# An expert's rows at every eighth of its 64 slots, in the place of one slot after the other

## What is computed

```python
def hier_moe(hn, w_group, w_expert, w_gate, w_up, w_down):
    pg = softmax(t @ w_group); g_sel = argmax(pg)            # one of 4 groups
    top_p, top_i = top_k(softmax(el_sel), 2)                 # two of its 8 experts
    comb = sum(one_hot(eid, 32) * w)                         # a weight for each token and expert
    for e in range(32):
        a = silu(t @ w_gate[e]) * (t @ w_up[e])
        out = out + comb[:, e:e + 1] * (a @ w_down[e])
```

## Time and profile before

| | us |
|---|---|
| median of 3 runs | 604.15 |
| lowest and highest | 602.49, 605.76 |
| the profiled execution | 599.2 |
| its span, first to last instruction | 597.4 |

### The profile page before, as it was taken

The page is one execution under the profiler, slowest core; times in us unless marked ns, Lnnn a source line. Parts: engine busy times, 40 slices in busy tenths (PEclk is TensorE's granted clock), DMA queues, the critical chain, the costliest instruction groups (busy, mean ns, idle before and its releaser), DMA issues.

```text
span 597.4 us, 7906 instructions
## 1 busy us (share of the span) xinstructions
PE 517.0 (87%) x2938; PEld 324.1 (54%) x2938; DVE 246.2 (41%) x576; ACT 144.6 (24%) x364; POOL 151.1 (25%) x287
## 2 busy tenths in 40 slices
PE   3597998999999999889995499999978787778895
PEld 3584776777777677568784463334333332333343
DVE  2857668869432465651225522122211101111337
ACT  4542344444635222232111100011000000000110
POOL 5064646203304444651102111111211101100000
PEclk9887997999999999999997589999988988888999
DMA  8521030022005922246926949999999999999884
GB/s 248 206 61 43 19 116 27 2 71 71 2 16 168 320 114 72 70 153 234 418 83 243 420 164 408 412 424 424 425 423 426 425 427 424 425 425 421 363 331 169
DMA packets 35031, 144.75 MB, mean 242 GB/s; under 512 B 5842, under 2 KB 8994, under 8 KB 23216
## 3 DMA queue, kind: packets, MB, share of 16 engines
q1 hardware_dynamic: 27440, 131.58, 55.9%
q0 software_dynamic: 4528, 9.01, 4.2%
q10 hardware_dynamic: 3024, 3.64, 1.8%
HBM read 138.16 MB, written 17.30 MB: 260 GB/s over the span
## 4 chain that ended last, share of the span: by engine, by line
PE 45%; SPq 21%; DVE 15%; issue 5%; ACT 4%; DMA 3%; POOL 2%; ACTq 0%; DVEq 0%; POOLq 0%
PE banks L940 18%; SPq L648 12%; PE banks L1162 7%; SPq L656 6%; DMA w_moe_a<-in_w_up_dram 3%; SPq L729 3%; PE banks L1177 3%; PE banks L1156 2%; PE banks L1115 1%; POOL w_lo L795 1%; PE banks L998 1%; PE banks L1083 1%; PE banks L1078 1%; DVE soft L1720 1%; PE banks L1250 1%
## 5 line engine op out<-in xcount | busy, mean ns | idle before, releaser
L795 POOL TENSOR_TENSOR w_lo<-w_raw,w_hi 128x512 fp32r<-128x512 f32 x52 | 69.1, 1347 | 124.1 <-ACT w_hi L1408 122.4
L1162 PE MATMUL banks<-w_moe_b,xgT 128*64 128x512 f32 x224 | 70.9, 659 | 16.4 <-DMA w_moe_b<-in_w_up_dram 10.5
L1162 PE MATMUL banks<-w_moe_a,xgT 128*64 128x512 f32 x224 | 68.1, 631 | 8.9 <-DMA w_moe_a<-in_w_up_dram 8.9
L940 PE MATMUL banks<-w_hi,xT_hi_a 128*128 128x512 f32 (+4 forms) x140 | 56.6, 404 | 7.0 <-ACT sv L1376 7.0
L1990 DVE SCALAR_TENSOR_TENSOR glu<-banks,wr,glu 128x256 f32<-128x256 f32 x15 | 7.3, 483 | 122.8 <-ACT glu L1537 122.8
L841 POOL DMA_INDIRECT y_d<-y_sb,idx x14 | 14.1, 1005 | 166.7 <-PE banks L1156 111.1
L940 PE MATMUL banks<-w_lo,xT_hi_a 128*128 128x512 f32 (+4 forms) x140 | 53.9, 385 | 0.0
L940 PE MATMUL banks<-w_hi,xT_lo_a 128*128 128x512 f32 (+4 forms) x140 | 53.6, 383 | 0.0
L1162 PEld LDWEIGHTS banks<-w_moe_b,xgT 128*64 128x64 f32 x224 | 22.4, 152 | 57.4 <-issue 54.7
L1537 ACT ACTIVATE glu<-banks,wr 128x256 f32<-128x256 f32 x15 | 7.1, 475 | 155.2 <-PE banks L1162 137.5
L940 PE MATMUL banks<-w_hi,xT_hi_b 128*128 128x512 f32 (+3 forms) x100 | 41.6, 416 | 0.4 <-POOL w_lo L795 0.4
(11 more groups left out here) (273 smaller groups left out, 888.7 us busy)
## 6 DMA issues: line engine op xcount, KB each, us to landing
w_moe_a<-in_w_down_dram SPq DMA_DIRECT2D x20, 1024.0 KB, 25.5
w_moe_a<-in_w_gate_dram SPq DMA_DIRECT2D x16, 1024.0 KB, 18.6
w_moe_a<-in_w_up_dram SPq DMA_DIRECT2D x16, 1024.0 KB, 21.5
w_moe_b<-in_w_gate_dram SPq DMA_DIRECT2D x14, 1024.0 KB, 24.1
w_moe_b<-in_w_up_dram SPq DMA_DIRECT2D x14, 1024.0 KB, 25.8
w_moe_b<-in_w_down_dram SPq DMA_DIRECT2D x12, 1024.0 KB, 24.8
w_raw<-in_w_in_dram SPq DMA_DIRECT2D x36, 256.0 KB, 4.6
y_d<-in_consts_dram SPq DMA_DIRECT2D x9, 512.0 KB, 10.3
```

Source lines behind the costliest of these rows:

```text
L795: nc.gpsimd.tensor_tensor(w_lo[:, s, :], w_raw[:, s, :], w_hi[:, s, :].bitcast(F32), ALU.subtract).then_inc(split, 1)
L940: l = mm(acc2[0:R, j % 2, 0:width], a[:, P * t:P * t + R], w, start=(kk == 0 and q == 0), stop=(kk == KD - 1 and q == 2))
L1162: l = mm(acc[64 * e:64 * e + 64, u, :].rearrange("p (m f) -> p m f", m=2), xgT[:, xu, k, 64 * e:64 * e + 64], units(at_e[e], 2)[:, :, k * ...
```

## The change

The one-hot table is made with another row of constants, `slots`, in the place of `iota`. In the slot s of an expert stands the number s % 8 * 8 + s // 8 + 1, so the row of rank r (from 0) goes to slot (r % 8) * 8 + r // 8: ranks 0 to 7 to slots 0, 8, ... 56, ranks 8 to 15 to slots 1, 9, ... 57, and so on. An expert with 36 rows filled slots 0 to 35; now it fills the slots 0 to 3 of each eight and in four of the eights slot 4 too. The row of constants takes the place of `ones`, and the second half of `counting` is now made by an operation on DVE.

```diff
@@ constants()
-    put("ones", np.ones((P, P)))
+
+    slot = p % CAP
+    put("slots", np.tile(p // CAP * CAP + slot % 8 * 8 + slot // 8 + 1, (P, 1)))
@@ stream_step()
-        ident, iota, ones = const("ident"), const("iota"), const("ones")
+        ident, iota, slots = const("ident"), const("iota"), const("slots")
@@ rows_factor(), DVE
-                step(nc.vector.tensor_copy(counting[:, :, :].rearrange("p a n -> p (a n)"), cst[:, lo:lo + 2 * P]))
+                step(nc.vector.tensor_copy(counting[:, 0, :], cst[:, lo:lo + P]))
+                step(ts(counting[:, 1, :], ident, 0.0, 1.0, ALU.mult, ALU.add))
@@ the one-hot tables, DVE (of the first pass, and in rows_of_level of the passes that these inputs do not need)
-                tt(row_oh[:, NT * h:NT * h + NT, :], iota.unsqueeze(1).to_broadcast([P, NT, P]),
+                tt(row_oh[:, NT * h:NT * h + NT, :], slots.unsqueeze(1).to_broadcast([P, NT, P]),
-                one(tt(row_oh[:, :, :], iota.unsqueeze(1).to_broadcast([P, 2 * NT, P]),
+                one(tt(row_oh[:, :, :], slots.unsqueeze(1).to_broadcast([P, 2 * NT, P]),
```

## The result

| | before | changed | changed / before, 95% interval |
|---|---|---|---|
| median of 4 runs each | 603.32 us | 614.54 us | 1.0186 (1.0153 to 1.022) |
| the profiled execution's span | 597.4 us | 612.2 us | |

The change costs 11.2 us. The direction, the mechanism and the range of the prediction hold; the forecast of 611.3 us put the loss at 7.2 us, and the rest of the study asks where the other four are.

What follows compares the result with a forecast made beforehand. The prediction took the most loaded of 16 DMA engines as the bound from 354 us on. Its one unhidden term, 47 rows x 0.154 = 7.2 us, on the median of 604.15 made 611.3 us; range 604.3 to 616.

Steps and rivals of the forecast that it cites:

- The bound: From 354 to 560 us all 16 DMA engines are busy; the most loaded one sets the last weights' landing and the end.
- Which partitions an engine serves: Read from a DMA share of 0.23 at the first two gathers' end, 343.80 to 344.40 us: four engines working on alone.
- the fours: Dealing rule taken: an engine serves four neighbouring partitions and the four 32 further on; the change then costs 7.2 us.
- eight neighbours: Rival: eight neighbouring partitions belong to one engine, so the change gains 12.8 us, to 591.4; chance 0.07.
- every sixteenth: Rival: every sixteenth partition belongs to one engine, so the change costs 10.3 us, to 614.5; chance 0.08.
- The rival without an engine limit: Memory or the way to it limits, not engines: no change, 604.3 us; chance 0.12, with cases adding up to 3 us.
- The price of a row: A 4 KB row costs its engine 0.154 us at 26.6 GB/s; empty slots cost nothing.
- The lower bound: Only 0.42 of the imbalance (2.9 of 6.9 us idle) reaches the end, so the added rows cost 3.0 us.
- The size of the sum: Most loaded engine, gathers 4 to 15 and scatters 0 to 13: 160 to 207 rows, 47 x 0.154 = 7.2 us.
- gathers 0 to 3 are done by then: Step leaving these gathers out of the row count, which starts at 354 us.
- The gathers and scatters, the operation on DVE, the last scatter: Longer transfers (1.9 us) and the DVE operation (0.2 to 0.3 us) hidden; last scatter and final 28 us unchanged.
- What was to be seen: Share near 0.5 before the last landing and in the first gathers; landing 7 us later; PE's waits 25 to 32 us.

Runs made afterwards that it cites:

- e3_one: Changed kernel, but one engine of each expert gets its full 8 rows in every transfer and the other seven share the rest; 1.018 of before.
- e2_round: Changed kernel, but each expert's ranks are dealt in turn to its eight engines (four partitions and the four 32 further on); 0.9928 of before.
- e6_rest: Changed kernel, but all experts except those of pairs 2 and 3 start at a later rank, which spreads them over all eight engines; 0.9955 of before.
- e7_round: The kernel of e2_round (ranks dealt in turn to the eight engines) once more, with more rounds; 0.995 of before.
- e5_start: Changed kernel, but the experts of pairs 2 and 3 alone start at rank 16, which spreads them over all eight engines; 1.0139 of before.
- e8_early: Changed kernel, but only the experts of pairs 4 to 8 are placed as in the change, all others spread; one run, 600.7 us (before 602.09).
- e9_late: Changed kernel, but only the experts of pairs 9 to 13 are placed as in the change, all others spread; one run, 602.25 us (before 602.09).
- e1_iota: Changed kernel with the slots filled in order again, the operation on DVE and the order of instructions kept; 0.9981 of before.

## Why the prediction was right

**The bound.** Right. The end of the stage follows the landing of the last weights, the tail behind it is 30.0 for 29.8 us, and e3_one shows that the most loaded of the 16 engines alone decides.

**Which partitions an engine serves.** The rule is right, but the stretch that it was read from does not carry it, and that the reading hit the right rule is in part luck. The fall does not end in two stretches of four engines; in the same view the share then rises again, before the last row has landed:

```profile
344.40:344.60 0.20, 0.20 (x3) 0.20 (x2) 0.00 (x0) 0.00 (x0) 0.00 (x0) 0.50 0.40 164
```

In the change the fall has no level at 0.5, and in e3_one, where by the fours two engines would work on alone for four rows (0.13), the share is 0.67, 0.64 and 0.21 from 347.5 to 348.4 us. So the share at the end of two gathers does not count the engines with rows left. What shows the rule is the whole runs: eight neighbours would have made the change a gain, every sixteenth would have made e2_round a loss, and e6_rest, which is faster than before, a loss of 10 us (208 rows for 141). The rival without an engine limit falls with e3_one, in which the same bytes take 11 us more.

**The price of a row.** 0.154 us was the calculated one. In the traces a packet of 4 KB of these transfers takes 0.159 us in the median and one of 8 KB of weights 0.309. Between e7_round and e5_start 75 rows make 11.8 us, 0.158 a row. An empty slot is not free, as the prediction has it, but nearly: it leaves a packet of 4 B, and that takes 9 ns.

**The lower bound.** The 3.0 us came from comparing 2.9 us of idle time up to 569.2 us with the 6.9 of the count. But the slowest engine is not done then. In every trace packets of 8 KB, which are the last down blocks, still run to 4.5 us behind the start of the last half, in the kernel before to 572.2. The comparison stopped before its end and says nothing of a lead that is lost.

**The size of the sum.** Too small: 7.2 us, and the stage grew by 10.9 to 11.3. One part is the step "gathers 0 to 3 are done by then". Gathers 2 and 3 were left out of the sum because they end before 354 us, but SP's loads for pair 3 queue behind them: with 15 rows on the most loaded engine the second of these lands 21.3 us behind the start of the one-hot matmuls, with 12 or 9 rows 18.7 to 19.0, and against 9 rows the stage is 1.9 us longer (e5_start). Why six rows cost that much more than their 0.9 us is open. Some 1.5 to 2 us remain, and they seem to lie with the kernel before: on a line of 0.158 us a row through e7_round its 160 rows would give 228.5, and its layout has 226.7 and 227.1 (e8_early and e9_late with 145 are 0.4 under that line). The same shows in the gain of e7_round, 3.8 us of stage for the counted 5.4. Why before is better than its rows was not tried.

**The range.** It held 614.5, and here too there is luck: its upper end, 616, was the 10.3 us of the wrong dealing, every sixteenth, and the spread of the runs. The change's 11.2 us are more than any loss that the prediction worked out.

**The gathers and scatters, the operation on DVE, the last scatter.** Hidden as said: the median landing of a gather went from 10.2 to 11.0 us and of a scatter from 8.3 to 8.6, and no wait of PE for a gather stands in its list; e1_iota gives the operation at nothing.

**What was to be seen.** The share near 0.5 before the last landing and under 1 before 560 us came; the level of 0.5 in the first gathers did not. The last landing came 11.3 us later in the place of 7. PE's waits before L1164 are 31.5 us for the 32 foretold, but that is a chance hit: they should have grown by the whole loss and grew by 6.3 of 11.3 us. The wait before L1306 grew by 1.3, and PE's busy time in the stage by 2.5 (200.8 for 198.2); a wait of 1.1 us for DVE (L1957) is new, and stands in e1_iota too.

## What to carry to other kernels

Where weights stream at the full rate of all DMA engines, as here, an indirect transfer costs what it adds to the most loaded engine, so deal its filled rows over the engines and not over the partitions: here partitions 4g to 4g+3 and the four that lie 32 further on belong to one engine, and rank r belongs on engine r % 8. A spread that looks even over partitions can put twice the rows on every second engine. A layout for which each way of dealing predicts a different sign tells them apart, as ranks dealt in turn did here; a few tenths of a microsecond at the end of a transfer do not.

## What was not expected of the hardware

The load behind gathers with a heavy engine came later than the added rows account for: with 15 rows in the place of 12 in gathers 2 and 3 it landed 9.6 in the place of 6.9 us after its issue (8.4 in e6_rest, also with 15). And a gain in the transfers can be taken back by the clock, or not, with the same kernel: in e2_round a wait of 3.49 us before the last half of gate and up was followed by 16 matmuls in 6.63 us at a granted 0.54, in e7_round one of 2.33 us by 3.65 us at full clock. What decides is open.
